# Attention stage of a two-block network: scores from split one-pass products, rotation on VectorE across rows, low parts of the weights on GpSimd

## What is computed

```python
q, k, v = jnp.split(h @ w_qkv, [q_w, q_w + kv_w], axis=-1)
q = _rms_norm(q.reshape(n_batch, n, SWA_HEADS, SWA_HEAD_DIM), q_gain)
k = _rms_norm(k.reshape(n_batch, n, SWA_KV_HEADS, SWA_HEAD_DIM), k_gain)
if rotate:
    q, k = _rope(q, cos, sin), _rope(k, cos, sin)   # x1*c - x2*s, x1*s + x2*c
...
s_ctx = jnp.einsum('bqhgd,bkhd->bhgqk', qb, kc)
s_win = jnp.where(allowed, jnp.einsum('bqhgd,bkhd->bhgqk', qb, kb), -jnp.inf)
p = _sink_softmax(jnp.concatenate([s_ctx, s_win], axis=-1), sink_hg)
return einsum(p[..., :ctx_len], vc) + einsum(p[..., ctx_len:], vb)   # then @ w_out
```

## Time and profile before

| | |
|---|---|
| median of 3 runs | 3080.75 us (3080.58 to 3081.11) |
| the profiled execution | 3080.93 us, its span 3079.1 us |
| TensorE busy | 3039.5 us (99%) |
| VectorE busy | 1895.3 us (62%) |
| ScalarE busy | 1320.9 us (43%) |
| GpSimd busy | 100.1 us (3%) |
| granted TensorE clock | 1.000 over the span |

### The profile page before, as it was taken

One profiled execution on the slowest core, in us unless ns is written; L12 is line 12 of the kernel. 1 busy time (PEld: TensorE's weight loads), 2 busy tenths in 40 slices (PEclk: granted clock), 3 DMA queues, 4 the chain that ended last, 5 costly groups with the idle time before them and its releaser, 6 DMA issues.

```text
span 3079.1 us, 52667 instructions
## 1 busy us (share of the span) xinstructions
PE 3039.5 (99%) x21054; PEld 2611.0 (85%) x21054; DVE 1895.3 (62%) x2808; ACT 1320.9 (43%) x2247; POOL 100.1 (3%) x106
## 2 busy tenths in 40 slices
PE   9999999999999999999999999999999999999999
PEld 8897889889888988888788788788887888886999
DVE  6745575675447656776777477467735676367544
ACT  5544454554345453222464567432224222255533
POOL 0000000100000020000000000100000000000000
PEclk9999999999999999999999999999999999999999
DMA  7543554454345543554422000235522454221453
GB/s 267 189 151 137 188 184 175 171 186 176 143 159 181 186 166 134 194 193 164 151 80 96 2 4 3 97 148 194 194 106 82 166 213 180 89 89 42 140 188 123
DMA packets 62488, 441.24 MB, mean 143 GB/s; under 512 B 6768, under 2 KB 8944, under 8 KB 9328
## 3 DMA queue, kind: packets, MB, share of 16 engines
q1 hardware_dynamic: 60992, 437.39, 38.9%
q10 hardware_dynamic: 1328, 1.46, 0.1%
HBM read 437.77 MB, written 1.05 MB: 143 GB/s over the span
## 4 chain that ended last, share of the span: by engine, by line
PE 90%; DVE 5%; ACT 3%; issue 1%; POOL 0%; DMA 0%; DVEq 0%; ACTq 0%; SPq 0%; POOLq 0%
PE ps_high L544 46%; PE ps_low L544 42%; PE ps_low L553 1%; DVE sb_w_split L834 1%; ACT sb_w_split L797 1%; DVE sb_arena L2215 0%; ACT sb_xn L2900 0%; ACT sb_arena L2909 0%; PE ps_high L553 0%; DVE sb_x_split L3003 0%; DVE sb_silu L3023 0%; DVE sb_arena L5056 0%; DMA sb_ring<-weights 0%; DVE sb_rinv L4960 0%; DVE sb_xn L4381 0%
## 5 line engine op out<-in xcount | busy, mean ns | idle before, releaser
L797 ACT ACTIVATE sb_w_split<-sb_ring 128x2048 fp32r<-128x2048 f32 x260 | 498.5, 1917 | 891.1 <-PE ps_low L544 697.9
L834 DVE TENSOR_TENSOR sb_w_split<-sb_ring,sb_w_split 128x2048 fp32r<-128x2048 f32 x260 | 597.6, 2298 | 255.7 <-ACT sb_w_split L797 255.7
L544 PE MATMUL ps_low<-sb_x_split,sb_w_split 128*128 128x512 f32 (+1 forms) x3640 | 709.2, 352 | 8.9 <-DVE sb_w_split L834 4.0
L544 PE MATMUL ps_high<-sb_x_split,sb_w_split 128*128 128x512 f32 (+1 forms) x3544 | 690.9, 353 | 0.3 <-DVE sb_w_split L834 0.3
L544 PEld LDWEIGHTS ps_low<-sb_x_split,sb_w_split 128*128 128x128 f32 x3640 | 595.1, 189 | 110.8 <-DVE sb_x_split L3003 6.3
L544 PEld LDWEIGHTS ps_high<-sb_x_split,sb_w_split 128*128 128x128 f32 x3544 | 583.7, 189 | 94.7 <-DVE sb_w_split L834 0.6
L544 PE MATMUL ps_low<-sb_a_split,sb_w_split 128*128 128x256 f32 (+1 forms) x2112 | 370.2, 325 | 0.3 <-DVE sb_w_split L834 0.3
L544 PE MATMUL ps_high<-sb_a_split,sb_w_split 128*128 128x256 f32 (+1 forms) x2112 | 365.7, 323 | 0.0
L544 PEld LDWEIGHTS ps_low<-sb_a_split,sb_w_split 128*128 128x128 f32 x2112 | 314.2, 190 | 37.9 <-DVE sb_w_split L834 2.6
L544 PEld LDWEIGHTS ps_high<-sb_a_split,sb_w_split 128*128 128x128 f32 x2112 | 314.9, 190 | 30.9
L1047 DVE SCALAR_TENSOR_TENSOR sb_rest<-sb_ring,sb_consts 128x1024 f32<-128x1024 f32 x256 | 313.3, 1224 | 26.0 <-DVE sb_rest L1047 6.2
(11 more groups left out here) (443 smaller groups left out, 3137.2 us busy)
## 6 DMA issues: line engine op xcount, KB each, us to landing
sb_ring<-weights SPq DMA_DIRECT2D x412, 1024.0 KB, 4.8
sb_consts<-consts SPq DMA_DIRECT2D x1, 2148.0 KB, 18.4
sb_sq<-xT SPq DMA_DIRECT2D x1, 1024.0 KB, 5.6
sb_ring<-weights SPq DMA_DIRECT2D x2, 512.0 KB, 7.6
sb_h<-ctxT ACTq DMA_DIRECT2D x1, 1024.0 KB, 14.4
out<-sb_h SPq DMA_DIRECT2D x1, 512.0 KB, 3.0
sb_vectors<-vectors ACTq DMA_DIRECT2D x1, 269.0 KB, 5.8
out<-sb_h SPq DMA_DIRECT2D x1, 256.0 KB, 2.7
```

The source lines that it names most:

```text
L544: ins = self.g.nc.tensor.matmul(out, lhsT, rhs, start=start, stop=stop)
L797: g.nc.scalar.activation(g.w_split[:, 0, s % 2, :], g.ring[:, n % SLOTS, :], ACT.Copy).then_inc(g.sem["w_high"], 1)
L834: g.nc.vector.tensor_tensor(g.w_split[:, 1, s % 2, :], g.ring[:, n % SLOTS, :], g.w_split[:, 0, s % 2, :].bitcast(F32), ALU.subtract).then ...
```

## The change

Three things at once.

- **Scores.** The rotated queries and keys are split into high and low parts (`turned_high` by ScalarE, `turned_low` by VectorE; queries into a half of `w_split`, keys into half of `a_split`), and `scores` issues for each query block three one-pass products for each of both heads, alternating between the heads, in place of one float32 product for each.
- **Rotation.** TensorE no longer takes part. VectorE multiplies 32 rows at a time by a signed sine and writes to the 32 rows beside them (`sin` is negated in the table for the second half), then multiplies all 128 rows by the cosine, then adds. `rotate_queries(0)` now comes ahead of `keys(0)`.
- **Low parts of the weights.** n = 3 to 11 go from VectorE to GpSimd (`swa_in_low_pool`); VectorE keeps 0 to 2.

In the list of TensorE the second and third value tile move: `value_tile(1)` comes ahead of `scores(0)`. The split of the output weights uses `w_split` for one of its three spaces.

```diff
+def swa_in_low_pool(pool, first, splits):
+    g = pool.g
+    pool.wait_ge(g.sem["swa_in_low"], 2)
+    for n in range(3, 2 * IN_CHUNKS):
+        chunk = first + n // 2
+        pool.wait_ge(g.sem["swa_in_high"], n + 1)
+        high, low = swa_in_split(g, splits, n)
+        ins = g.nc.gpsimd.tensor_tensor(low, half_source(g, chunk, n), high.bitcast(F32), ALU.subtract)
...
-    def rotated_queries(n):
-        pe.wait_ge(g.sem["high_free"], pe.tiles["high"] - 3)
-        for half in range(2):
-            side, count = evicted[2 * n + half]
-            pe.wait_ge(g.sem[side + "_free"], count)
-        rotation(b["q"][:, 2 * n:2 * n + 2, :])
...
-        pe.wait_ge(g.sem["rotated"], pe.due("rotated", {0: 3, 4: 1, 6: 1}.get(p, 0)))
+        pe.wait_ge(g.sem["turned_low"], pe.due("turned_low", {0: 3, 4: 1, 6: 1}.get(p, 0)))
...
-                pe.mm(tiles[i][:, :], b["q"][base:base + SWA_DIM, p, q * P:(q + 1) * P],
-                      b["k"][base:base + SWA_DIM, kv // 2, :], True, False)
+            for n, (q_part, k_part) in enumerate(((0, 0), (0, 1), (1, 0))):
+                for i, head in enumerate(swa_pairs()[p]):
+                    rows, kv = slice(SWA_DIM * i, SWA_DIM * (i + 1)), head // (SWA_HEADS // SWA_KV)
+                    pe.mm(tiles[i][:, :], split_queries(g, pe.splits, q_part)[rows, p, q * P:(q + 1) * P],
+                          split_keys(g, k_part)[rows, kv // 2, :], n == 0, False)
...
     queries(3)
-    pe.wait_ge(g.sem["high_free"], pe.tiles["high"] - 3)
-    pe.wait_ge(g.sem["dn_normed"], pe.due("dn_normed", 2))
-    rotation(b["k"][:, :, 0:TOK])
     query_lengths(1)
     value_tile(0)
+    value_tile(1)
     scores(0)
-    value_tile(1)
-    rotated_queries(2)
     value_tile(2)
-    rotated_queries(3)
     value_tile(3)
...
+    turned_queries(0)
+    turned_queries(1)
+    query_root(1)
+    act.wait_ge(g.sem["turned"], act.due("turned"))
+    A(split_keys(g, 0), b["k"], ACT.Copy).then_inc(g.sem["turned_high"], 1)
...
+    def rotate(raw):
+        other = b["tmp"]
+        for at in range(0, P, ROTATED):
+            to, rows = slice(at, at + ROTATED), slice(at ^ ROTATED, (at ^ ROTATED) + ROTATED)
+            v.tensor_tensor(other[to, :, :], raw[rows, :, :], both(sin)[rows, :, :],
+                            ALU.mult).then_inc(g.sem["vec_step"], dve.adds("vec_step"))
+        dve.wait_ge(dve.last_sem, dve.last_count)
+        v.tensor_tensor(raw, raw, both(cos), ALU.mult).then_inc(g.sem["vec_step"], dve.adds("vec_step"))
+        dve.wait_ge(dve.last_sem, dve.last_count)
+        v.tensor_tensor(raw, raw, other, ALU.add).then_inc(g.sem["turned"], dve.adds("turned"))
...
+    rotate_queries(0)
     keys(0)
     keys(1)
-    rotate_queries(0)
     query_scales(0)
-    swa_in_low(dve, 9, dve.chunks, dve.splits)
     rotate_queries(1)
-    for n in (10, 11):
-        swa_in_low(dve, n, dve.chunks, dve.splits)
-    rotate([b["k"][:, m, 0:TOK] for m in range(2)])
+    rotate(b["k"][:, :, 0:TOK])
+    low_queries(0)
+    low_queries(1)
     query_scales(1)
+    turned_low(2, split_keys(g, 0), split_keys(g, 1), b["k"])
```

More of the change, by code:

```diff
@@ L4590, in swa_out_split, with split_queries, split_keys @@
         return [g.x_split[:, 0, :, TOK + part * P:TOK + (part + 1) * P] for part in range(2)]
-    return [g.a_split[:, 2 - space, part, :, :].rearrange("p a (b n) -> p (a b) n", n=P) for part in range(2)]
+    if space == 1:
+        return [g.w_split[:, part, 1 - splits % 2, 0:CHUNK // 2].rearrange("p (k n) -> p k n", k=KT) for part in range(2)]
+    return [g.a_split[:, 0, part, :, :].rearrange("p a (b n) -> p (a b) n", n=P) for part in range(2)]
+def split_queries(g, splits, part):
+    return g.w_split[:, part, splits % 2, :].rearrange("p (n t) -> p n t", n=PAIRS)
+def split_keys(g, part):
+    return g.a_split[:, 1, part, :, :]
 def swa_out_high(act, n, first):
@@ L4606, in swa_out_low @@
     dve.wait_ge(g.sem["swa_out_high"], n + 1)
-    high, low = swa_out_split(g, n)
+    high, low = swa_out_split(g, dve.splits, n)
     ins = g.nc.vector.tensor_tensor(low, half_source(g, chunk, n), high.bitcast(F32), ALU.subtract)
@@ L4628, in pairs @@
     def pairs(n, tile, which):
-        w = swa_out_split(g, n)
+        w = swa_out_split(g, pe.splits, n)
         for p in which:
@@ L4652, in swa_tensor @@
     norm_rows_tensor(pe, BOTH)
-    first, squares, evicted = pe.chunks, swa_squares(b), {}
+    first, squares = pe.chunks, swa_squares(b)
     def in_ready(n):
@@ L4668, in part_of, with open_query @@
         return [part[:, k, :] for part in w]
-    def open_query(n, side):
+    def open_query(side):
         pe.wait_ge(g.sem[side + "_free"], pe.tiles[side] - 3)
-        evicted[n] = (side, pe.tiles[side] + 1)
         return pe.open(side)
@@ L4676, in queries @@
         for half in range(2):
-            w, tile = in_ready(2 * n + 2 + half), open_query(2 * n + half, "low")
+            w, tile = in_ready(2 * n + 2 + half), open_query("low")
             for k in range(KT):
@@ L4720, in swa_tensor @@
     key_tiles = [pe.open("low"), pe.open("low")]
-    query_tiles = [open_query(0, "low"), open_query(1, "high")]
+    query_tiles = [open_query("low"), open_query("high")]
     stream_tensor(pe, key_tiles[0], 3)
@@ L4858, in key_root, with query_root @@
         A(g.root[:, :], tile[:, :], ACT.Sqrt, scale=1.0 / SWA_DIM, bias=g.eps[:, 0:1]).then_inc(g.sem["root"], act.adds("root"))
-    def query_root(half, skipped):
-        act.skip("high", skipped)
+    def query_root(half):
         act.wait_ge(g.sem["high_full"], act.tiles["high"] + 1)
@@ L4942, in swa_vector @@
     norm_rinv_vector(dve, BOTH)
-    norm_low_vector(dve, 1, BOTH, late=True,
-                    between=lambda k: swa_in_low(dve, 3 + k // 4, dve.chunks, dve.splits) if k in (0, 4) else None)
-    for n in range(5, 9):
-        swa_in_low(dve, n, dve.chunks, dve.splits)
+    norm_low_vector(dve, 1, BOTH, late=True)
+    queries_low, queries_high = dve.freed["low"] + 2, dve.freed["high"]
     dve.skip("low", PAIRS + 1)
@@ L4949, in swa_vector, with both @@
     cos, sin = g.const("swa_cos"), g.const("swa_sin")
+    def both(table):
+        return table.rearrange("p (o t) -> p o t", o=1).to_broadcast([P, 2, TOK])
     def length(parts, gain):
@@ L4967, in length, with turned_low, low_queries @@
                 ins.then_inc(g.sem["vec_step"], dve.adds("vec_step"))
[L4969 to L4987 removed]
+    def rotate(raw):
[4 more added lines that the diff above has]
+                            ALU.mult).then_inc(g.sem["vec_step"], dve.adds("vec_step"))
+        dve.wait_ge(dve.last_sem, dve.last_count)
+        v.tensor_tensor(raw, raw, both(cos), ALU.mult).then_inc(g.sem["vec_step"], dve.adds("vec_step"))
+        dve.wait_ge(dve.last_sem, dve.last_count)
+        v.tensor_tensor(raw, raw, other, ALU.add).then_inc(g.sem["turned"], dve.adds("turned"))
+        dve.wait_ge(dve.last_sem, dve.last_count)
+    def turned_low(n, high, low, raw):
+        dve.wait_ge(g.sem["turned_high"], n + 1)
+        v.tensor_tensor(low, raw, high.bitcast(F32), ALU.subtract).then_inc(g.sem["turned_low"], 1)
+    def low_queries(n):
+        pair = slice(2 * n, 2 * n + 2)
+        high, low = (split_queries(g, dve.splits, part)[:, pair, :] for part in range(2))
+        turned_low(n if n < 2 else n + 1, high, low, b["q"][:, pair, :])
     def keys(m):
@@ L5001, in rotate_queries @@
     def rotate_queries(n):
-        rotate([b["q"][:, 2 * n + half, :] for half in range(2)])
+        if n == 0:
+            dve.wait_ge(g.sem["high_free"], queries_high + 1)
+        dve.wait_ge(g.sem["low_free"], queries_low + max(1, 2 * n + 1))
+        rotate(b["q"][:, 2 * n:2 * n + 2, :])
     if dve.foreign["high"]:
```

63 lines of the change are left out of this document (25 added, 38 removed).

## The result

| | before | changed |
|---|---|---|
| median of 6 runs each, on one chip | 3081.27 us (3080.58 to 3082.53) | 3093.22 us (3092.84 to 3094.3) |
| ratio | | 1.0038, 95% interval 1.0029 to 1.0048 |
| the profiled execution | 3080.93 us, span 3079.1 | 3093.24 us, span 3091.4 |
| granted TensorE clock, mean | 1.000 | 0.997 |

The changed kernel is 12.0 us slower; the forecast was 7.6 us slower, 3088.5 us, with a range of 3077 to 3094. So the measured time lies in the range, 0.8 us from its upper end.

What follows compares the result with a forecast made beforehand. TensorE, busy in 99% of the span, was taken as the bound, with VectorE becoming it ahead of the loop. +10.3 us there and -2.7 in the loop gave +7.6 on 3080.93: 3088.5 us, range 3077 to 3094.

Steps and rivals of the forecast that it cites:

- The forecast's path: Ahead of the loop, GpSimd and VectorE shut each other out when both read two SBUF operands: +10.3 us in all.
- First rotation and norm: Ahead of the keys' reciprocals: GpSimd collisions cost +1.4 us in the norm and +6.8 us at the first rotation.
- Scaling of the second key row: Ahead of the loop, one of its two VectorE instructions waits while GpSimd works on n = 11: +2.4 us.
- Finishing line at full clock: VectorE's eviction of the first transposes, at 2799.51 before, ends the part ahead of the loop: +10.3 us there.
- VectorE without GpSimd: From 2769.55 to the first evicted transposes, VectorE's 29.96 us become 29.6 without gaps, making it the bound: -0.3 us.
- A rotation: Six VectorE instructions at 0.69 us, nothing overlapping as each changes partitions: 4.34 us in place of 2.31.
- The loop: One-pass score blocks take 0.80 us, not 1.06; 0.45 us saved a pair over six pairs: -2.7 us.
- rival 3: TensorE's clock falls to 1.2 GHz after waits of 4.5 to 7 us: +3.5 us, 3092; chance 0.17.
- the waits before it hiding the rest: At TensorE's lower clock only the loop would lose; slower work ahead of it would cost nothing.
- The sum: Whole kernel: +10.3 ahead of the loop, -2.7 in it, +7.6 us on 3080.93: 3088.5 us.
- Rival 1: At the first rotation, GpSimd does not shut VectorE out or is waited for once: 3078 to 3082 us; chance 0.20.
- Rival 2: In the scores, one-pass products don't pair, a block takes 1.41 us: 3096.6 us; chance 0.08.

Runs made afterwards that it cites:

- 23 dummy products: Changed kernel plus unread dummy TensorE work in three idle times (14 products, 23 products ahead of the first scores, 24 transposes): 3089.81 us against 3081.03 before.
- with the clock kept: Changed kernel plus unread dummy TensorE work in three idle times (14 products, 13 ahead of the first scores, 24 transposes): 3090.99 us against 3081.98 before.
- the kernel with the low parts back: Changed kernel with all low parts of the weights made by VectorE again, VectorE's rotation and one-pass scores staying: 3087.92 us against 3081.05 before.

## Why the prediction was right, and where it was off

The forecast's path, GpSimd shutting VectorE out ahead of the loop, held from point to point. The time came out 4.4 us above it: 3.2 of them are the clock, by the prices above, and the rest I can't assign. The clock was named as a rival and not counted; the range held with 0.8 us to spare.

- **First rotation and norm.** Forecast: the keys' reciprocals 7.9 us late (1.1 + 6.8). Measured 7.88. TensorE's wait in the norm 1.3 forecast, 1.41 measured; the rotation's six instructions were said to end at 2768.9, and ended at 2770.44, less the 1.6 us by which this execution came late.
- **Scaling of the second key row.** Forecast +2.4, measured 2.75 - 0.88 = 1.9. GpSimd was done with n = 11 at 2780.31, which is 2778.7 less the 1.6, 0.4 sooner than forecast, and the scaling got through before its recorded end.
- **Finishing line at full clock.** Forecast +10.3 in all, measured 9.5 with 23 dummy products. The forecast's own terms make 10.0: the norm's delay was 1.1, and the 0.3 by which the sum makes it +1.4 are a gain without GpSimd that no other term takes in, since the -0.3 of VectorE's sum is counted from 2769.55 on, behind the norm. With 1.9 in place of 2.4 for the scaling, 10.0 becomes the 9.5 measured; so nothing is left over for VectorE's sum without gaps.
- **VectorE without GpSimd.** The -0.3 us at the finishing line that the text gives for this holds only with the low parts gone from VectorE; no run has them gone and GpSimd idle. The nearest run, all of them on VectorE, has +6.1; less 3.4 for n = 9 to 11 and 2.8 for the late reciprocals that is -0.1.
- **A rotation.** 4.34 us taken, 4.3 measured; four products that change partitions don't overlap (2.83 us for four, where the page shows 0.69 for one). With the rule of the Trainium skill (VectorE: DVE Perf Modes, section Two Vector instructions with no wait between them), that an instruction which starts in another quadrant than the last one waits for all earlier ones, this trace agrees.
- **The loop.** The mis-sized term: a block of scores was to take 0.80 us and takes 0.90, so it saves 0.16 us and not 0.26. A pair saves 0.33 us instead of 0.45; with the clock kept, the six pairs save 2.0 instead of 2.7 (11.3 to 9.3 between the finishing lines of pairs 0 and 7).
- **The clock.** The step that failed is the placing of rival 3: it stood beside the forecast as an alternative with a chance of 0.17, though its condition, waits of 4.5 to 7 us, was part of the forecast itself. It should have been a term of the sum. Its size, 3.5 us for half a pair, was nearly right in total (1.7 + 1.5 = 3.2), by luck, and wrong in place: "the waits before it hiding the rest" didn't hold for the first scores, for which VectorE waited 2.19 and 0.90 us. The waits were also shorter (3.72, 2.85 and 4.68 us, for 4.7, 4.5 and 7): the last two since the slow stretches ahead of them filled part, the first with nothing slow ahead of it, for which I have no reason. What the Trainium skill says (TensorE: Matmul & The Clock Gate, section Part 1: The HAM clock gate), that an idle array falls to 1.2 GHz, could not be shown from before; after, the rows at 0.50 and 0.55 agree.
- **The sum.** 9.5 - 2.0 = 7.5 without the clock, against 7.6 forecast. That it is so near is luck: the finishing line was forecast 0.8 too late and the loop's gain 0.7 too large. With the clock it was 10.7 at the end of the profiled execution. The medians differ by 12.0; the rest of 1.3 is less than the two arrival times differ named at the top, and I can't assign it further.
- **Rivals.** Rival 1 (no lock-out) fell, by the alternation above and by the kernel with the low parts back. Rival 2 (the products don't pair) fell: 0.90 us and not 1.41.

## What to carry to other kernels

Before work is moved to GpSimd, look at what VectorE runs in that very moment: beside an instruction with one operand in SBUF the move was free and brought its full worth, beside instructions with two it made the kernel 5 us slower, although nine subtractions had left the engine that was the bound. Parts that are each hidden in the same idle time have no prices that add: +3.3, -1.2 and +0.2 us alone made +12.0 together. And if a forecast contains waits of TensorE of several microseconds, the slower clock behind them is a term of it wherever someone waits for that work, not a rival.
